# Constant products in TensorE's waits, and the mixers' first rows loaded and gated in the latent attention

## The reference, cut to what matters

```python
for l in range(DEPTH):
    shift, scale, gate = jnp.split(c_act @ ada_w[l] + ada_b[l], 3, axis=-1)
    h = rms_norm(x, norm_w[l]) * (1.0 + scale[:, None, :]) + shift[:, None, :]
    proj = h @ w_in[l]
    ...
    r_o = rms_norm(retention(rope(rq), rope(rk), rv))
    m_o = mla(mq, mkv, mkr, ...)
    g_o = rms_norm(gla(gq, gk, gv, gg, gla_w_g2[l], gla_b_g2[l]), gla_norm[l])
    mixed = jnp.concatenate([r_o * silu(rz), m_o * silu(mz), g_o * silu(gz)], axis=-1)
    x = x + gate[:, None, :] * (mixed @ w_out[l])
return rms_norm(x, final_norm)
```

## Time and profile before

| | |
|---|---|
| median of 3 runs | 3963.51 us (3962.93 to 3965.69) |
| the profiled execution | 3960.46 us, its span 3958.6 us |
| TensorE busy | 87% of the span |
| VectorE, ScalarE, GpSimd busy | 59%, 47%, 8% |
| mean granted clock of TensorE | 0.928 |

### The profile page before, as it was taken

One profiled execution on the slowest core, in us unless ns is written; L12 is line 12 of the kernel. 1 busy time (PEld: TensorE's weight loads), 2 busy tenths in 40 slices (PEclk: granted clock), 3 DMA queues, 4 the chain that ended last, 5 costly groups with the idle time before them and its releaser, 6 DMA issues. The chain is left out here.

```text
span 3958.6 us, 52447 instructions
## 1 busy us (share of the span) xinstructions
PE 3433.7 (87%) x17759; PEld 2707.0 (68%) x17759; DVE 2344.4 (59%) x3718; ACT 1876.4 (47%) x3141; POOL 315.6 (8%) x379
## 2 busy tenths in 40 slices
PE   8988979599999789759999990999895979989778
PEld 7876658488887546657888870778674757877556
DVE  3226656799988666458999875540334745213276
ACT  3115651387888510117788871321445623224374
POOL 0000001000001110000000103000002200000032
PEclk9999989699999899879999995999997989999879
DMA  6322224399999764609999986441213344212232
GB/s 239 102 70 64 70 94 168 130 398 398 399 398 399 290 261 171 229 29 379 399 399 398 399 331 221 152 158 62 55 46 127 104 147 166 94 54 54 86 117 79
DMA packets 409755, 785.41 MB, mean 198 GB/s; under 512 B 99424, under 2 KB 154360, under 8 KB 407544
## 3 DMA queue, kind: packets, MB, share of 16 engines
q1 hardware_dynamic: 386552, 699.35, 49.0%
q0 software_dynamic: 13824, 50.34, 3.5%
q10 hardware_dynamic: 9216, 33.56, 2.1%
HBM read 647.19 MB, written 135.95 MB: 198 GB/s over the span
## 5 line engine op out<-in xcount | busy, mean ns | idle before, releaser
L225 DVE TENSOR_TENSOR experts_gate_lo<-weights_gate,experts_gate_hi 128x1024 fp32r<-128x1024 f32 x256 | 299.2, 1221 | 58.8 <-ACT experts_gate_hi L221 57.9
L225 DVE TENSOR_TENSOR experts_down_lo<-weights_down,experts_down_hi 128x1024 fp32r<-128x1024 f32 x256 | 301.8, 1221 | 53.8 <-ACT experts_down_hi L221 51.3
L221 ACT CAST experts_gate_hi<-weights_gate 128x1024 fp32r<-128x1024 f32 x256 | 255.0, 1055 | 114.8 <-PEq L126 67.8
L225 DVE TENSOR_TENSOR experts_up_lo<-weights_up,experts_up_hi 128x1024 fp32r<-128x1024 f32 x256 | 296.1, 1218 | 1.2 <-ACT experts_up_hi L221 0.5
L272 PE MATMUL project_acc<-project_wh,project_hh 128*128 128x512 f32 (+2 forms) x768 | 285.6, 372 | 0.0
L274 PE MATMUL project_acc<-project_wh,project_hl 128*128 128x512 f32 (+2 forms) x768 | 282.0, 367 | 0.0
L273 PE MATMUL project_acc<-project_wl,project_hh 128*128 128x512 f32 (+2 forms) x768 | 281.8, 367 | 0.0
L221 ACT CAST experts_down_hi<-weights_down 128x1024 fp32r<-128x1024 f32 x256 | 257.0, 1052 | 30.5 <-DMA weights_down<-in_moe_w_down_dram 30.2
L221 ACT CAST experts_up_hi<-weights_up 128x1024 fp32r<-128x1024 f32 x256 | 254.8, 1057 | 8.8 <-DMA weights_up<-in_moe_w_up_dram 7.5
L2456 ACT COPY project_row<-project_acc 128x512 f32<-128x512 f32 (+2 forms) x96 | 51.9, 541 | 379.4 <-PE project_acc L274 379.4
L272 PE MATMUL experts_yp<-experts_down_hi,experts_hTh 128*128 128x512 f32 x512 | 209.9, 410 | 13.0 <-DVE experts_hTl L225 13.0
(11 more groups left out here) (453 smaller groups left out, 8077.8 us busy)
## 6 DMA issues: line engine op xcount, KB each, us to landing
weights_gate<-in_moe_w_gate_dram SPq DMA_DIRECT2D x256, 512.0 KB, 13.2
weights_up<-in_moe_w_up_dram SPq DMA_DIRECT2D x256, 512.0 KB, 12.3
weights_down<-in_moe_w_down_dram SPq DMA_DIRECT2D x256, 512.0 KB, 11.7
scratch_y<-experts_y ACTq DMA_DIRECT2D x64, 512.0 KB, 6.3
pool_shared<-in_ada_w_dram SPq DMA_DIRECT2D x16, 1536.0 KB, 6.8
project_raw<-in_w_in_dram SPq DMA_DIRECT2D x8, 2048.0 KB, 9.5
scratch_proj<-project_row SPq DMA_DIRECT2D x64, 256.0 KB, 2.0
qkv_raw<-in_attn_w_qkv_dram SPq DMA_DIRECT2D x48, 256.0 KB, 3.2
```

The costliest lines, as they stand in the source:

```text
L221: return act.copy(hi, src)
L225: return dve.tensor_tensor(lo, src, hi.bitcast(F32), ALU.subtract)
```

## The change

It does two things.

First, a helper `keep_warm` issues n plain FP32 products of the identity with 512 columns of constants (`K["warm"]`, a view of the constants' tile) into a PSUM bank that holds nothing of use at that moment. It has no waits of its own. It is called in TensorE's stream at the ends of the phases qkv, attention, experts, pool, project and (layer 0) mixout, at the starts of attention, out, experts, pool, project, and in route and mixout at the start and between their steps. `phase_route` gets a PSUM bank for it.

Second, a class `MixAhead`, a `Phase` around the latent attention and the mixers of each layer, holds the raw buffers of the output weights (five instead of four), the small tensors, the row, value and gate (`zs`) buffers. SP loads the rows and values of tiles 0 and 1, the gate weights, bias and norm, and the first five chunks of the output weights inside the latent attention, and ScalarE computes the SiLUs of tiles 0 and 1 at that phase's end. In the mixers, the output gate and the final norm get a semaphore of their own, waited for by VectorE before the first residual; the weights' splits are indexed in the order of use, and the first `project` waits for them one by one; tiles 0 and 1 are interleaved up to the states, the second with a PSUM bank of its own (`small_bank`) and with `elast` doubled.

```diff
+def keep_warm(nc, K, bank, n):
+    for _ in range(n):
+        nc.tensor.matmul(bank, K["ident"], K["warm"], start=True, stop=True)
...
# phase_qkv, TensorE, at the end
                 each_chunk(pe, chunk)
+                keep_warm(nc, K, tp[:, 1, :, :].rearrange("p a b -> p (a b)"), 5)
...
# phase_attention, SP
                 load_q(1)
                 load_v(1)
+                if prefetch:
+                    prefetch.load_first(nc, sp)
                 for h in range(HEADS):
...
+                    if prefetch and h + 2 < prefetch.RAWS:
+                        prefetch.load_w(sp, h + 2)
# phase_attention, TensorE
+                spare = tp[:, :, :].rearrange("p a b -> p (a b)")
+                keep_warm(nc, K, spare, 3)
                 turn("k", 0, 0)
...
                 narrow_outputs(N - 1)
+                keep_warm(nc, K, spare, 3)
# phase_attention, ScalarE, at the end
+                if prefetch:
+                    for i in range(2):
+                        prefetch.silus(act, i)
...
# phase_out_norm, TensorE
+                keep_warm(nc, K, lg[:, 0, :], 9 if heads else 3)
                 transpose_x(0)
+                if not heads:
+                    keep_warm(nc, K, lg[:, 0, :], 4)
                 pe.wait_ge(x_lo, 2)
                 (the first tile's products)
+                keep_warm(nc, K, lg[:, 0, :], 4)
                 pe.wait_ge(small_in, 16 * 6)
# phase_route, TensorE
+                keep_warm(nc, K, spare[:, :], 10)
                 pe.wait_ge(m_ready, 1)
                 (three products)
+                keep_warm(nc, K, spare[:, :], 16)
                 pe.wait_ge(ab_ready, 1)
# phase_experts, TensorE
+                keep_warm(nc, K, spare, 5)
                 transpose_x(0, 0)
...
                 transpose_h(n * 2 + 1)
+                keep_warm(nc, K, spare, 6)
                 down(n * 2 + 1)
+                keep_warm(nc, K, spare, 3)
# phase_combine_pool: 8 before m.turn_vectors, 4 at the end
# phase_project: 7 before and 7 after transposes(0), 3 at the end
...
+class MixAhead(Phase):
+    RAWS = 5
+    def load_first(self, nc, sp):
+        for n in range(2):
+            self.load_w(sp, n)
+        (g2, bg, gn: three loads, small_in)
+        for i in range(2):
+            self.load_row(sp, i)
+            self.load_vv(sp, i)
+    def silus(self, act, i):
+        act.wait_ge(self.row_in[i % 2], 16 * len(self.SEGS) * (i // 2 + 1))
+        for c, at in (("rz", 0), ("gz", 256), ("mz", HALF)):
+            z = self.col(i, c)
+            last = act.activation(self.zs[:, i % 2, at:at + z.shape[-1]], z, ACT.Silu)
+        last.then_inc(self.silu_done, 1)
...
# phase_mix_out, SP: its first loads
+                load_mo(0)
+                load_mo(1)
+                sp.dma_start(gate[:, :], mod[2:3, :].partition_broadcast(P)).then_inc(gate_loaded, 16)
                 if final:
+                    sp.dma_start(fn[:, :], final_norm.partition_broadcast(P)).then_inc(gate_loaded, 16)
+                load_x(0)
                 load_row(2)
+                for n in range(ahead.RAWS, KC):
+                    sp.wait_ge(w_lo_ready, n - ahead.RAWS + 1)
+                    ahead.load_w(sp, n)
# phase_mix_out, TensorE: ahead of the loop
                 open_tile(0)
+                keep_warm(nc, K, spare, 2)
                 gate_and_retention(0)
                 open_tile(1)
+                keep_warm(nc, K, spare, 3)
+                gate_and_retention(1)
+                keep_warm(nc, K, spare, 2)
                 gla_scores(0)
                 updates(0)
-                gate_and_retention(1)
-                for i in range(T):
+                keep_warm(nc, K, acc[1][:, :], 5)
+                gla_scores(1)
+                outputs(0)
+                open_tile(2)
+                updates(1)
+                gate_and_retention(2)
+                mixed_transposes(0)
+                for i in range(1, T):
# phase_mix_out, ScalarE: ahead of the loop
-                copies(0); softplus(0); split 0; exponents(0); splits 1-3; copies(1); silus(0), silus(1); splits 4, 5
+                copies(0); softplus(0); copies(1); exponents(0); softplus(1); exponents(1); splits 0-4;
+                take_outputs(0); copies(2); splits 5-7; silus(2)
# phase_mix_out, VectorE: ahead of the loop
+                gate_in(0); retention_scores(0); gate_sums(0); gate_in(1); retention_scores(1)
+                gla_operands(0); gate_sums(1); gla_parts(0); states(0); gla_operands(1)
+                splits 0-3
+                gla_parts(1); mean_squares(0); gated(0); states(1); normalized(0)
+                splits 4-7
```

More of the change, by code:

```diff
@@ L501, in _, with phase_attention @@
                     angles.reduce(dve)
-def phase_attention(nc, K, name, q, k, v, out, maps, dk, dv, mask, scale, totals, lam_parts=None):
+def phase_attention(nc, K, name, q, k, v, out, maps, dk, dv, mask, scale, totals, lam_parts=None, prefetch=None):
     PAIRS = TILES // 2
@@ L856, in with_constants @@
         at += a.shape[1]
+    K["warm"] = held[:, 0:HALF]
     SETTLED.append(nc.alloc_semaphore("settled"))
@@ L2571, in _, with mla_attention @@
                         finish_mla(j)
-def mla_attention(nc, K, name, mq, mk, mkv, out, totals):
+def mla_attention(nc, K, name, mq, mk, mkv, out, totals, ahead):
     def tiles(ap, base, step, width):
@@ L2590, in phase_mix_out @@
+def phase_mix_out(nc, K, name, ahead, mla_o, x, mod, final_norm, out):
     T = TILES
     final = final_norm is not None
-    SEGS = (("rq", "rk"), ("rz", "rz"), ("mz", "gk"), ("gg", "gz"))
+    SEGS = ahead.SEGS
     at, col_at = 0, {}
@@ L2622, in phase_mix_out @@
         ms, rs, half = ph.sb("ms", [P, 8]), ph.sb("rs", [P, 8]), ph.sb("half", [P, 8])
[L2623 removed]
+        zs, silu_done, mixed = ahead.zs, ahead.silu_done, ph.sb("mixed", [P, 2, D])
         mh, ml = ph.sb("mh", [P, KC, P], F32R), ph.sb("ml", [P, KC, P], F32R)
@@ L2639, in phase_mix_out @@
             "acc_ready", "x_part", "x_added", "sums_ready", "fs_ready", "fr_ready", "xn_ready", "rqw_ready", "rkw_ready",
-            "silu_done", "zg_ready", "set_up", "own", "act_own"))
-        row_in, v_in, stored = ([ph.sem(f"{n}{b}") for b in range(2)] for n in ("row_in", "v_in", "stored"))
+            "zg_ready", "set_up", "own", "act_own"))
+        mo_in, stored = ([ph.sem(f"{n}{b}") for b in range(2)] for n in ("mo_in", "stored"))
         def col(i, n):
@@ L2906, in _ @@
                 project(T - 1, 1)
+                if not final:
+                    keep_warm(nc, K, tA[:, :, :].rearrange("p a b -> p (a b)"), 3)
             @block.scalar
@@ L2977, in row_sums, with split_hi @@
                     act.activation(junk[:, :], xn[:, i % 2, :], ACT.Square, accum_out=fs[:, 0:1]).then_inc(sums_ready, 1)
+                def split_hi(n):
+                    act.wait_ge(raw_in, 16 * ahead.RAWS if n < ahead.RAWS else 16 * KC)
+                    part_hi(act, w_hi[:, n, :], raw[:, n % ahead.RAWS, :]).then_inc(w_hi_ready, 1)
                 copies(0)
                 softplus(0)
-                w.split_hi(act, 0)
+                copies(1)
                 exponents(0)
-                for k in range(1, 4):
-                    w.split_hi(act, k)
-                copies(1)
-                silus(0)
-                silus(1)
-                for k in range(4, 6):
-                    w.split_hi(act, k)
-                for i in range(T + 2):
+                softplus(1)
+                exponents(1)
+                for n in range(5):
+                    split_hi(n)
+                take_outputs(0)
+                copies(2)
+                for n in range(5, KC):
+                    split_hi(n)
+                silus(2)
+                for i in range(1, T + 2):
                     if has(i - 1):
@@ L2996, in _ @@
                         softplus(i + 1)
-                    if i == 0:
-                        for k in range(6, KC):
-                            w.split_hi(act, k)
                     if has(i):
@@ L3017, in gate_in @@
                     dve.wait_ge(rs_ready, i + 1)
-                    ch(dve.tensor_scalar(z[:, :], sc[:, 3, :], bg[:, 0:1], None, ALU.add))
+                    ch(dve.tensor_scalar(z[:, :], small_bank(i)[:, 3, :], bg[:, 0:1], None, ALU.add))
                     ch.wait()
@@ L3125, in _ @@
                 gate_sums(0)
-                w.split_lo(dve, 0)
+                gate_in(1)
+                retention_scores(1)
                 gla_operands(0)
-                w.split_lo(dve, 1)
+                gate_sums(1)
                 gla_parts(0)
-                w.split_lo(dve, 2)
                 states(0)
-                for i in range(T + 2):
+                gla_operands(1)
+                for n in range(4):
+                    split_lo(n)
+                gla_parts(1)
+                mean_squares(0)
+                gated(0)
+                states(1)
+                normalized(0)
+                for n in range(4, KC):
+                    split_lo(n)
```

(8 more changed lines are left out.)

186 lines of the change are left out of this document (104 added, 82 removed).

## The result

| | before | changed |
|---|---|---|
| median | 3964.53 us (3962.93 to 3965.69, 4 runs) | 3898.17 us (3895.78 to 3901.69, 4 runs) |
| profiled execution, span | 3960.46, 3958.6 us | 3897.70, 3895.9 us |
| TensorE busy, mean granted clock | 87%, 0.928 | 92%, 0.968 |

The ratio is 0.9834, with a 95% interval of 0.9817 to 0.9851: 66 us faster. Run again beside later experiments, the changed kernel took 3900.44 us (3898.07 to 3905.70, 5 runs), at a ratio of 0.9838 (0.9824 to 0.9851).

What follows compares the result with a forecast made beforehand. TensorE, 87% busy, bounds the kernel, the rest being waits between stages and the low clock after them. 43.8 (mixers) + 20 (clock) - 0.8 (barriers) = 63 us gained, so 3900.5 us; range 3876 to 3930.

Steps and rivals of the forecast that it cites:

- The mixers' term: Mixers' start to first output product: 41.5 us instead of 60.5 and 66.3, VectorE's queue last; gain 43.8 us.
- the clock's term: Constant products in TensorE's waits: 24.0 us from attention, experts and pool, less 4 for held-up work; net 20.
- The bound below it, 32 us with serial chains: Mixers' start: tiles' chains stay serial, only loads go, 32 us; as rival with half the clock's gain 3921, chance 0.09.
- The prefetch hidden: Latent attention: 17 DMA issues, about 8 us, cost nothing; rival, not hidden: 5 us a layer, 3910, chance 0.03.
- what the Trainium skill: ScalarE's table loads: about 2.7 us each instead of 1.28, gain some 13 us smaller; rival at double weight 3913, chance 0.03.
- The 0.8 us for two more barriers: The extra scope around attention and mixers: one more barrier a layer, 0.4 us each, 0.8 us lost.
- nothing from the rest: Out, project and routing stages: no clock gain counted, as most of these places keep gaps of 2 us and more.
- the prediction's sign: Attention's first scores: at 1.6 us in the changed profile, against 3.78 before, if the clock is warm.
- That constant products raise the clock: Every burst: such products raise the clock, 0.86 us each at full clock in most bursts, 1.84 at the low one.
- The slower rival: Every burst: constant products don't raise the clock, cost near 105 us in all, 4025 us; chance 0.04.

Runs made afterwards that it cites:

- experiment 3: The changed kernel with two of the eight low parts of the output weights computed by GpSimd in place of VectorE: 3909.44 us, ratio 0.9863.
- experiment 4: The changed kernel with tile 0's low parts moved ahead on VectorE and tile 2's SiLUs behind tile 0's high parts on ScalarE: 3897.45 us, ratio 0.9829.
- experiment 2: The changed kernel without the four bursts (12 constant products) in each mixer's start, all others kept: 3903.84 us, ratio 0.9849.
- Experiment 8: The changed kernel's loads and SiLUs ahead, but the mixers in the order of before and without constant products in their start: 3904.67 us, ratio 0.9856.
- `ahead_only`: The changed kernel without any constant product: 3926.26 us, ratio 0.9901.
- `warm_only`: The kernel before with all constant products but the 12 in each mixer's start; loads, SiLUs and mixers' order as before: 3941.13 us, ratio 0.9943.
- `pool_splits`: Same run as experiment 3: the changed kernel with two low parts of the output weights on GpSimd, 3909.44 us.
- `serial_order`: Same run as Experiment 8: the changed kernel's loads ahead, the mixers' order of before, no constant products in their start, 3904.67 us.
- `few_places`: Same run as Experiment 6: the changed kernel with constant products in qkv, attention, experts and pool stages alone, 3910.45 us.
- `rows_late`: The changed kernel with rows, values and SiLUs of tiles 0 and 1 back in the mixers, order and bursts as changed: 3921.21 us, ratio 0.9886.
- `doubled`: Same run as experiment 10: the changed kernel with every burst doubled, 3991.41 us.
- `mixers_cold`: Same run as experiment 2: the changed kernel without the 12 constant products in each mixer's start, 3903.84 us.
- `short_starts`: Same run as experiment 7: the changed kernel with shorter bursts at the starts of the experts and the second out stage, 3910.43 us.
- Experiment 6: The changed kernel with constant products in the qkv, attention, experts and pool stages alone, 63 of 200: 3910.45 us, ratio 0.9865.
- experiment 10: The changed kernel with every burst doubled, 400 constant products: 3991.41 us, ratio 1.0066.
- experiment 5: The kernel of experiment 4 with one constant product in each of TensorE's two waits before the first output product: 3892.63 us, ratio 0.9818.
- experiments 3 and 9: The runs `pool_splits` (3909.44 us) and `rows_late` (3921.21 us), in that order.
- experiment 7: The changed kernel with the burst at the experts' start cut from 5 to 3 and the second out stage's from 3 to 2: 3910.43 us, ratio 0.9852.

## Why the prediction was right

The forecast was 3900.5 us and 63 us gained against its profile; measured were 3898.2 and 62.7. The mixers' term was right by its mechanism; the clock's term was right in its sum by luck. Step by step:

- **The mixers' start, 43.8 us: right**, 44.8. The gate product came at 4.3 us (forecast 4.1), tile 1's operands at 22.4 and 23.2 (21.7), and VectorE's queue from there took 18.1 and 18.3 us (19.8, as the splits took 9.7 and 9.2 us, not 11.6), so the first output product came at 40.5 and 41.5 (41.5). That VectorE's queue sets the last 20 us is shown by its 19 us of work in them, and from two sides: the product got 3.1 and 4.3 us later when VectorE was slowed (experiment 3) and 2.7 and 4.0 us sooner when work was taken from in front of it (experiment 4). What the prediction did not have is that ScalarE has its part of the mixed tile ready only 0.2 to 0.3 us before VectorE gets to it. A lower clock of TensorE moves the product by only 1.2 us (experiment 2).
- **The bound below it, 32 us with serial chains: too low.** It priced the loads at the wait for the gate vector plus 4.5 us. Experiment 8 measured 38.3 without the new order, at a partly lower clock. The loads carry the part, not the interleaving.
- **The prefetch hidden: right.** From the attention's last product to the mixers' start took 3.96 us after as 3.95 before, with two tiles' SiLUs and a table load in it; and no attention grew, also without constant products (215.1 and 215.6 us in `ahead_only`, from the first product of its own to the last, 216.2 before in both layers). The table load is 1.28 us again (2972.95 to 2974.24), and the SiLU behind it starts at 2974.25: what the Trainium skill ("ScalarE: Activation LUTs", "What ACT_TABLE_LOAD costs") would have added isn't there. The 0.8 us for two more barriers can't be seen by itself; the waits ahead of the stages grew by some 0.5 together.
- **Not foreseen: some is given back later.** Layer 1 takes 147.9 us from its first output product to its last, where it took 144.7. The prediction put nothing there. The first output products are at the lower clock, which adds 1.5 us, and the clock falls again 1.2 us behind the wait of 1.83 us ahead of the last tile's, 1.7. Other kernels with this loop bear it out: with no such fall the stretch, to the end of its last product, took 145.1 to 145.2 us (before, `warm_only`, `pool_splits`, `serial_order`), with one 146.7 to 146.8 (`few_places`, `rows_late`, `doubled`), with two 148.1 to 148.3 (the changed kernel in both profiles, `ahead_only`, `mixers_cold`, `short_starts`).
- **The clock, 20 us net: right in sum, wrong in its places.** The prediction took 24.0 from attention, experts and pool, nothing from the rest, and 4 off. Measured in the first profile: attention 8.3, not 11.9, since the clock falls again before the first scores (3.78 us, where the prediction's sign was 1.6); experts 9.2 within (forecast 10), 3.2 of which are lost again to bursts that run past the rows' arrival; pool none; but project 4.0, out 2.5 and routing 2.2, which were counted at zero. Experiment 6 puts those and the mixers' at 10 us. So the step "nothing from the rest" failed, and a shortfall in the places that were counted hid it: attention, experts and pool brought 14.3 net (8.3 + 9.2 - 3.2) where the prediction had 20, and the other three 8.7. Of these 23.0, 5.1 went in the qkv stage, behind the mixers' first product and in waits, which leaves the 17.9 beside the mixers' start.
- **That constant products raise the clock: right.** 200 of them at 1.01 us stand between 0.86 and 1.84, and most bursts at 0.87 to 0.95. Alone they bring 23 us, beside the mixers' part up to 28 (3926.3 to 3898.2, two sets of runs).
- **The slower rival** did not come, and experiment 10 shows its place is real: at twice the length the bursts cost more than they bring.

In the first out stage most of the gain was made and given back: the first tile's products ran 3.1 us ahead of before up to 577.9, and then waited 2.2 us for a low part of the weights:

```profile
584.33 0.80 PE L1019 MATMUL out_acc<-out_w_hi,out_xh 128*128 128x512 f32 x1 [2.21 <-DVE out_w_lo L262]
```

Open: whether the 1 to 3 us a stage between two profiles with the same code there come only from where the clock falls. In the second layer's mixers they do, by the stretches above; for the other stages it was not worked out, and no run held the clock fixed.

## What to carry to other kernels

Time spent on a stage's first loads can be removed by issuing them, and whatever needs nothing else, one stage earlier; here that was worth 38 us, more than the order of the work and a warm clock together, and it held at either clock. After that, read which engine's queue ends last and which ends just before it, and move what isn't needed yet (the last weights' parts, the next tile's gate) behind the operation that the next engine waits for. Constant products paid here where they ended as the real operand arrived; what ran past it was paid (3.2 us at the experts, 91 us when all were doubled). They did not help across a chain of short waits behind them (the first attention), where one product inside each wait did (experiment 5). Work moved to another engine or another time can slow the engine beside it: look at what GpSimd does while VectorE sets the pace.

## What was not expected of the hardware

- A subtraction of 128x1024 on VectorE takes 1.22 us alone and 3.4 beside one of GpSimd's (2.65 and 3.32 there); an operation of 0.28 us took 2.44. VectorE's operation ended 1.08, 0.55 or 0.15 us, by its size, behind GpSimd's each time (experiments 3 and 9), so they seem to take turns and not to share. Spreading such work over both was slower than VectorE alone.
- A wait of 1.8 us was followed by the lower clock in one profile and not in another of nearly the same kernel (experiment 7), and stages with the same code differ by 1 to 3 us between profiles (the pool stage 2.0 us, the first mixers behind their first product 2.9, in two profiles of the changed kernel); a gain of that size is read from one stage's own operations, not from the total.
- The lower clock costs little where TensorE waits: without the constant products the whole start of the mixers ran at 0.62 and took 1.3 to 2.1 us longer, of 42.
